# Two gate projections cut into twelve pieces and set between the products of a chunk scan

## What is computed

```python
q_a, k_a, v_a, z_a, b_a, a_a, q_b, k_b, v_b, g_a, g_b = split(h @ w_in)
o_a = gated_delta_rule(l2norm(silu(conv(q_a))), l2norm(silu(conv(k_a))), silu(conv(v_a)), g, beta)
o_a = rmsnorm(o_a, gdn_norm_w) * silu(z_a)
o_b = sliding_window_sink_attention(rope(q_b), rope(k_b), v_b, sinks)
y = sigmoid(g_a) * (o_a @ w_a_out) + sigmoid(g_b) * (o_b @ w_b_out)
x = x + gt1 * (y @ w_mix_out)
...
def step(state, chunk):            # the chunk scan: 4 chunks of 64 tokens, 4 heads
    v_new = u_c - w_c @ state
    o = qd @ state + a_c @ v_new
    state = state * exp(gl) + kd.T @ v_new
```

## Time and profile before

| | |
|---|---|
| time, median of 3 runs | 1943.98 us (1943.7 to 1944.88) |
| profiled execution | 1944.16 us |
| its span (first to last record) | 1942.4 us |
| mean clock of TensorE | 0.971 of full speed |
| PE busy | 1794.1 us, 92% |
| PEld busy | 1494.5 us, 77% |
| DVE busy | 1513.9 us, 78% |
| ACT busy | 1085.4 us, 56% |
| chain that ended last | PE 76%, DVE 13%, ACT 6%, issue 3% |

### The profile page before, as it was taken

One profiled execution on the slowest core, in us unless ns is written; L12 is line 12 of the kernel. 1 busy time (PEld: TensorE's weight loads), 2 busy tenths in 40 slices (PEclk: granted clock), 3 DMA queues, 4 the chain that ended last, 5 costly groups with the idle time before them and its releaser, 6 DMA issues.

```text
span 1942.4 us, 25749 instructions
## 1 busy us (share of the span) xinstructions
PE 1794.1 (92%) x9708; PEld 1494.5 (77%) x9708; DVE 1513.9 (78%) x1475; ACT 1085.4 (56%) x917; POOL 88.6 (5%) x139
## 2 busy tenths in 40 slices
PE   3988998899998989998799999999999999999996
PEld 1877877788887878876587787877878778788785
DVE  6768937977756667446788898898988989888888
ACT  2563215433333472232677777777777777877774
POOL 4010000000000010001000000000000010000100
PEclk9999989999999999898899999999999999999999
DMA  9525744788873414224699999999999999999994
GB/s 302 179 87 183 230 129 152 245 297 301 279 243 109 152 44 109 85 71 148 245 375 352 387 355 370 364 359 378 355 373 372 357 372 365 360 378 364 352 370 174
DMA packets 261719, 520.78 MB, mean 268 GB/s; under 512 B 12202, under 2 KB 75924, under 8 KB 261652
## 3 DMA queue, kind: packets, MB, share of 16 engines
q1 hardware_dynamic: 257988, 506.21, 73.7%
q0 software_dynamic: 3664, 13.63, 1.8%
HBM read 511.42 MB, written 8.39 MB: 268 GB/s over the span
## 4 chain that ended last, share of the span: by engine, by line
PE 76%; DVE 13%; ACT 6%; issue 3%; SPq 1%; DMA 0%; DVEq 0%; ACTq 0%
PE bank L964 17%; PE bank L965 17%; PE bank L966 17%; PE bank L970 6%; PE bank L971 5%; PE bank L972 5%; DVE w_lo L1508 2%; DVE ada_acc L1529 2%; DVE w_lo L2042 2%; ACT w_hi L933 2%; PE bank L1456 1%; PE bank L984 1%; ACT w_hi L691 1%; PE bank L1229 1%; PE bank L1203 1%
## 5 line engine op out<-in xcount | busy, mean ns | idle before, releaser
L2042 DVE TENSOR_TENSOR w_lo<-ring,w_hi 128x2048 fp32r<-128x2048 f32 x336 | 768.3, 2291 | 118.2 <-ACT w_hi L933 114.8
L933 ACT CAST w_hi<-ring 128x2048 fp32r<-128x2048 f32 x336 | 640.0, 1910 | 131.7 <-PE bank L966 131.6
L964 PE MATMUL bank<-w_hi,xg_hi 128*128 128x512 f32 x896 | 358.6, 400 | 23.1 <-DVE w_lo L2042 23.1
L966 PE MATMUL bank<-w_hi,xg_lo 128*128 128x512 f32 x896 | 353.8, 395 | 0.0
L965 PE MATMUL bank<-w_lo,xg_hi 128*128 128x512 f32 x896 | 353.8, 395 | 0.0
L970 PE MATMUL bank<-hT_hi,w_hi 128*128 128x256 f32 x960 | 282.3, 294 | 12.9 <-DVE w_lo L1508 6.3
L1508 DVE TENSOR_TENSOR w_lo<-ring,w_hi 128x2048 fp32r<-128x2048 f32 x96 | 219.5, 2290 | 87.5 <-ACT w_hi L691 87.3
L971 PE MATMUL bank<-hT_lo,w_hi 128*128 128x256 f32 x960 | 274.7, 286 | 0.0
L972 PE MATMUL bank<-hT_hi,w_lo 128*128 128x256 f32 x960 | 274.4, 286 | 0.0
L691 ACT CAST w_hi<-ring 128x2048 fp32r<-128x2048 f32 x96 | 182.3, 1901 | 81.7 <-PE bank L966 45.5
L964 PEld LDWEIGHTS bank<-w_hi,xg_hi 128*128 128x128 f32 x896 | 168.8, 188 | 67.6 <-issue 21.2
(11 more groups left out here) (393 smaller groups left out, 2071.4 us busy)
## 6 DMA issues: line engine op xcount, KB each, us to landing
ring<-in_moe_w_gate_dram SPq DMA_DIRECT2D x112, 1024.0 KB, 7.1
ring<-in_moe_w_up_dram SPq DMA_DIRECT2D x112, 1024.0 KB, 7.4
ring<-in_moe_w_down_dram SPq DMA_DIRECT2D x112, 1024.0 KB, 7.4
ring<-in_ada_w_dram SPq DMA_DIRECT2D x48, 1024.0 KB, 5.6
ring<-in_w_in_dram SPq DMA_DIRECT2D x38, 1024.0 KB, 5.1
ring<-in_ffn_w_gate_dram SPq DMA_DIRECT2D x14, 1024.0 KB, 6.3
ring<-in_ffn_w_up_dram SPq DMA_DIRECT2D x14, 1024.0 KB, 5.1
ring<-in_ffn_w_down_dram SPq DMA_DIRECT2D x14, 1024.0 KB, 5.4
```

The lines of the kernel that those rows point to most:

```text
L933: act.copy(w_hi[p % NS_MOE][:], ring[:, p % RING, :]).then_inc(hi_ready, 1)
L964: pe.matmul(o, xh, wh, start=start, stop=False)
L966: return pe.matmul(o, xl, wh, start=False, stop=stop)
L2042: dve.tensor_tensor(w_lo[p % NS_MOE][:], ring[:, p % RING, :], f32(w_hi[p % NS_MOE][:]), ALU.subtract).then_inc(taken, 1)
```

## The change

Gates 6 and 7 are cut into twelve pieces (`gate_piece`) of 9 or 6 matmuls. Eight stand in the scan, one or two for each chunk, and four behind it; `wb 0` now stands wholly behind the scan. The two outputs of gates 6 and 7 go to banks 0 and 3 instead of both to bank 0, which shifts the banks of `wb 1`, the mix product and `gate_row`. The output products of a chunk are no longer alternated: a small product of zeros clears the bank, then come the four from the state and the four from `v_new`. On VectorE and ScalarE the splits move: gate 7's stands ahead of the scan, `wb 0`'s behind it, `wa 0`'s on ScalarE behind the rounding of `oa_hi`. In layer 0 the last six adaLN units move from between gates 5, 6 and 7 to behind `wb 0`, `wb 1` and `wa 0`, and with them their passes, their small products, `ada_turn` and `gate_diag`. `gate_row` moves from ahead of `wa 0` to between the two halves of the mix product, `gate_copy` behind the splits. On ScalarE a table set that holds both Ln and Exp is loaded ahead of them, twice in each mixer.

```diff
@@ units @@
             if l == 0:
-                ada_units(1 if j < 3 else 2)
+                ada_units((1, 1, 1, 2, 2, 0, 0, 0)[j])
         for cc in range(2):
             units.append((("wb", l, cc), True))
+            if l == 0:
+                ada_units(2)
         for cc in range(2):
             units.append((("wa", l, cc), True))
+            if l == 0 and cc == 0:
+                ada_units(2)
@@ ScalarE @@
+                act.preload_act_table_set("natural_log_exp_and_others")
...
+                ahead(("gate", l, 7), 0)
                 for n in range(NCH):
...
-                    if n == 0:
-                        ahead(("gate", l, 7), 0)
-                    if n in (1, 2):
-                        gate(5 + n)
-                        ahead(("wb", l, 0), 0)
...
+                    if n == 2:
+                        gate(6)
                 act.wait_ge(o_s, NCH * (l + 1))
                 act.activation(o_sq, OT, ACT.Square).then_inc(osq_s, 1)
-                if l == 0:
-                    ada_copy(2, 1)
+                ahead(("wb", l, 0), 0)
+                act.wait_ge(split_used, s_of[("gate", l, 7)] + 1)
+                act.activation(gate_sb[:, 14:16, :].rearrange("p a b -> p (a b)"),
+                               ps[3][:], ACT.Sigmoid).then_inc(gate_s, 1)
                 ahead(("wb", l, 1), 0)
+                act.preload_act_table_set("natural_log_exp_and_others")
                 act.wait_ge(on_ps, l + 1)
...
                 act.activation(o_r, o_r, ACT.Exp, scale=-0.5).then_inc(on_s, 1)
-                ahead(("wa", l, 0), 0)
                 act.wait_ge(oaf, l + 1)
                 act.copy(oa_hi[:], OT).then_inc(oa_h, 1)
+                ahead(("wa", l, 0), 0)
                 ahead(("wa", l, 1), 0)
+                if l == 0:
+                    ada_copy(2, 1)
@@ TensorE @@
+                def gate_piece(i):
+                    late, piece = divmod(i, 6)
+                    t, third = divmod(piece, 3)
+                    wh, wl = parts(("gate", l, 6 + late), KO)
+                    if piece == 0 and not late:
+                        pe.wait_ge(gate_s, 8 * l + 6)
+                    for ko in ((0, 1, 2), (3, 4, 5), (6, 7))[third]:
+                        ins = by_channel(ps[(0, 3)[late]][:, t * T:(t + 1) * T], wh[:, ko, t * P:(t + 1) * P],
+                                         wl[:, ko, t * P:(t + 1) * P], hT_hi[:, ko, :], hT_lo[:, ko, :],
+                                         ko == 0, ko == KO - 1)
+                    if piece == 5:
+                        ins.then_inc(split_used, 1)
...
-                        meanwhile(0)
+                        gate_piece(2 * n)
...
-                    meanwhile(1)
+                    gate_piece(2 * n + (n > 0))
...
+                    if n:
+                        pe.matmul(ps[7][:, 0:T], zero_b[:, 0:P], zero_b[:], start=True, stop=False)
+                        for h in range(H):
+                            pe.matmul(ps[7][:, h * CHUNK:(h + 1) * CHUNK], state[:, h, :], qT[:, h, here],
+                                      start=False, stop=False)
                     for h in range(H):
-                        o = ps[7][:, h * CHUNK:(h + 1) * CHUNK]
-                        if n:
-                            pe.matmul(o, state[:, h, :], qT[:, h, here], start=True, stop=False)
-                        ins = pe.matmul(o, v_new[rows, h, :], AT[rows, tb * H + h, rows], start=n == 0, stop=True)
+                        ins = pe.matmul(ps[7][:, h * CHUNK:(h + 1) * CHUNK], v_new[rows, h, :],
+                                        AT[rows, tb * H + h, rows], start=n == 0, stop=n == 0 or h == H - 1)
                     ins.then_inc(o_ps, 1)
-                    if l == 0 and n in (0, 2):
-                        ada_piece(0, 9 + n // 2, 1, False, False)
+                    if n == 0:
+                        gate_piece(1)
+                gate_piece(8)
+                gate_piece(9)
 
                 pe.wait_ge(osq_s, l + 1)
...
+                gate_piece(10)
+                gate_piece(11)
+                half_branch("wb", 0, (2, 3), ob_hi, ob_lo, 0)
                 pe.wait_ge(gate_s, 8 * (l + 1))
+                half_branch("wb", 0, (2, 3), ob_hi, ob_lo, 1)
                 if l == 0:
-                    pe.wait_ge(ada_s, 2)
-                branch("wb", 1, (0, 1), ob_hi, ob_lo)
-                pe.wait_ge(yb_s, 4 * l + 1)
-                gate_row(2 * l + 1, m_dg, (2, 3))
+                    ada_piece(0, 9, 1, False, False)
+                half_branch("wb", 1, (0, 5), ob_hi, ob_lo, 0)
+                pe.wait_ge(ln2_s, 2 * (l + 1))
+                half_branch("wb", 1, (0, 5), ob_hi, ob_lo, 1)
+                if l == 0:
+                    ada_piece(0, 10, 1, False, False)
                 pe.wait_ge(oa_s, l + 1)
                 branch("wa", 0, (6, 7), oa_hi, oa_lo)
...
+                        if kh == 0 and cc == 1:
+                            gate_row(2 * l + 1, m_dg, (3, 1))
@@ VectorE @@
+                ahead(("gate", l, 7), 0)
                 for n in range(NCH):
...
-                    if n == 0:
-                        ahead(("gate", l, 7), 0)
...
-                        if n == 1:
-                            ahead(("wb", l, 0), 0)
...
                 ahead(("wb", l, 0), 0)
-                if l == 0:
-                    ada_columns(2, 0, 1, NQA, NQ)
-                    dve.wait_ge(ada_s, 2)
                 dve.wait_ge(gate_s, 8 * (l + 1))
                 dve.wait_ge(o_ps, NCH * (l + 1))
-                gate_diag(2 * l + 1, l, 2, m_dg)
+                ahead(("wb", l, 1), 0)
                 gated(1, 0, (2, 3), y_sum[:, 0:4, :])
-                ahead(("wb", l, 1), 0)
...
-                gate_copy(2 * l + 1, m_gt, (2, 3))
...
+                if l == 0:
+                    ada_columns(2, 0, 1, NQA, NQ)
+                    dve.wait_ge(ada_s, 2)
+                gate_diag(2 * l + 1, l, 2, m_dg)
+                ahead(("mix", l, 1, 1), 0)
+                gate_copy(2 * l + 1, m_gt, (3, 1))
```

More of the change, by code:

```diff
@@ L187, in build_program @@
         am1 = sb("am1", [P, 2 * P], BF16)
+        zero_b = sb("zero_b", [P, T], BF16)
         cols = sb("cols", [P, 2 * P])
@@ L584, in _ @@
             pool.memset(prm_b, 0.0).then_inc(zeroed, 1)
+            pool.memset(zero_b[:], 0.0)
             pool.memset(eps_c[:], EPS)
@@ L840, in gate @@
                 def gate(j):
-                    product(("gate", l, j))
+                    product(("gate", l, j), 1 if j < 6 else 0)
                     act.activation(gate_sb[:, 2 * j:2 * j + 2, :].rearrange("p a b -> p (a b)"),
@@ L1255, in _ @@
                     state = states[n % 2]
-                    def meanwhile(t):
-                        if n in (1, 2):
-                            if t == 0:
-                                pe.wait_ge(gate_s, 8 * l + 5 + n)
-                            one_block(("gate", l, 5 + n), 0, t)
-                        if n == 3:
-                            half_branch("wb", 0, (2, 3), ob_hi, ob_lo, t)
                     if n > 0:
@@ L1307, in _ @@
                 ins.then_inc(on_ps, 1)
+                gate_piece(10)
+                gate_piece(11)
+                half_branch("wb", 0, (2, 3), ob_hi, ob_lo, 0)
                 pe.wait_ge(gate_s, 8 * (l + 1))
+                half_branch("wb", 0, (2, 3), ob_hi, ob_lo, 1)
                 if l == 0:
-                    pe.wait_ge(ada_s, 2)
-                branch("wb", 1, (0, 1), ob_hi, ob_lo)
-                pe.wait_ge(yb_s, 4 * l + 1)
-                gate_row(2 * l + 1, m_dg, (2, 3))
+                    ada_piece(0, 9, 1, False, False)
[4 more added lines that the diff above has]
+                    ada_piece(0, 10, 1, False, False)
                 pe.wait_ge(oa_s, l + 1)
                 branch("wa", 0, (6, 7), oa_hi, oa_lo)
-                branch("wa", 1, (4, 5), oa_hi, oa_lo)
+                if l == 0:
+                    ada_piece(0, 11, 1, False, True)
+                half_branch("wa", 1, (4, 5), oa_hi, oa_lo, 0)
                 pe.wait_ge(yb_s, 4 * l + 2)
-                pe.wait_ge(gt_s, 2 * l + 1)
+                half_branch("wa", 1, (4, 5), oa_hi, oa_lo, 1)
+                if l == 0:
+                    ada_turn(2, 1)
                 for kh in range(2):
@@ L1325, in _ @@
                                 ko = 4 * kh + kk
-                                ins = by_token(ps[2 * cc + tb][:], hT_hi[:, ko, tokens(tb)], hT_lo[:, ko, tokens(tb)],
+                                ins = by_token(ps[(0, 2, 6, 7)[2 * cc + tb]][:], hT_hi[:, ko, tokens(tb)], hT_lo[:, ko, tokens(tb)],
                                                wh[:, kk, :], wl[:, kk, :], ko == 0, ko == KO - 1)
@@ L1852, in _ @@
                 dve.tensor_tensor(oa_lo[:], OT, f32(oa_hi[:]), ALU.subtract).then_inc(oa_s, 1)
-                gated(1, 1, (0, 1), y_sum[:, 4:8, :])
+                gated(1, 1, (0, 5), y_sum[:, 4:8, :])
                 ahead(("wa", l, 1), 0)
```

(3 more changed lines are left out.)

4 lines of the change are left out of this document (removed).

## The result

| | before | changed |
|---|---|---|
| median | 1943.84 us (1942.19 to 1944.88, 4 runs) | 1918.06 us (1917.06 to 1918.78, 4 runs) |
| span of the profiled execution | 1942.4 us | 1916.5 us |
| mean clock of TensorE | 0.971 | 0.980 |

The ratio is 0.9869 (95%: 0.9857 to 0.9881), 25.8 us less. I had said 1933, in a range of 1923 to 1939, so the kernel is 4.9 us faster than the range allowed.

What follows compares the result with a forecast made beforehand. The two mixers bound it: TensorE delayed by too-thick filling in the scans, then ScalarE and VectorE behind them. Layer 1 -5.0, layer 0 -3.4 and table loads -2.6 made -11.0 us: 1933 us, range 1923 to 1939.

Steps and rivals of the forecast that it cites:

- two falls in each scan: Both layers' scans: TensorE's clock falls twice in each as before, 1.5 us each, so 3.0 per scan.
- The fall at 821: Layer-1 scan before the change: clock at 1.2 GHz for 3.2 us without idle time ahead, taken as evidence against rival A.
- Rival A: Clock stays up in filled scans with denser outputs; five to six falls saved, -20 us, 1924; chance 0.25.
- The one fall in each tail: Idle time ahead of wa 0 and layer 0's gaps waiting for VectorE cost one clock fall each, 1.5 us.
- Prices: Scan products at full clock: output group 2.3 us (2.91 before), state product 1.31; chunk 7.87 instead of 14.2.
- The ends of the tails: Layer 0: mix product at 314.0, VectorE's chain ending at 312; layer 1: 12.2 us from wa 0, plus 1.5 for the clock.
- Table loads: Normalisation: Ln and Exp in one set take one 1.28 us load per mixer off the path, 2.6 us in all.
- the second load lies beside VectorE's two passes: Normalisation: the other removed load, that of L784, is hidden, so only 1.28 us per mixer counts.
- the new wait of 4.5 us: Layer 1's tail: TensorE waits 4.5 us before wa 0, whose split now stands behind ScalarE's rounding.
- VectorE as the bound of layer 0's tail: Layer 0 behind the scan: moved adaLN passes, splits and other VectorE work make 36.3 us; mix product at 309, not 319.1.
- Rival B: Layer 0 gives nothing, through weight transfers landing late or a longer VectorE chain: -6 to -7 us, 1937; chance 0.15.
- Rival C: Scan mostly at 1.2 GHz because thin pieces leave TensorE less dense: 1967, middling case some 1950; chance 0.04.

Runs made afterwards that it cites:

- three small moves: Changed kernel with wa 0's split ahead of the rounding, layer 1's gate row ahead of wa 0, two adaLN pairs in layer 0's scan: 1907.4 us together.
- One program: Changed kernel with output products alternated by head again, without the zero product: 1935.08 us, ratio 0.9959, ten runs.

## Why the prediction was wrong in size

The side, the places and the new waits came as forecast. The sum was -11.0 and the spans differ by 25.9. The missing 14.9 us, in spans, by its own steps (15.1 by the rounded parts):

1. **The clock (the step that failed): 6.0 in the scans.** I took two falls in each scan at 1.5 each, because "update, outputs and state product ... remain the sort of work after which the clock fell". None came. The fall at 821 followed the alternated outputs, not these products as such: grouped outputs alone take it away with everything else as before, and alternated outputs bring falls back in scans without idle time. Rival A described the right case for the scans, at 0.25, but its -20 took the tails' falls away too, and those came; with only the four falls of the scans gone it would have said 1927. The runs add that filling is the second condition: without it grouped outputs don't hold the clock. The one fall in each tail came as forecast; from wa 0 to the mix product layer 1 took 14.3 us, where 12.2 and 1.5 were forecast, and 11.9 without the fall, so that one cost 2.4.
The Trainium skill ("TensorE: Matmul & The Clock Gate", HAM oscillation) puts such falls down to idle gaps. The unfilled scans here agree (0.61 in the window of the version without filling), though their gaps of 0.67 and 0.78 us are much shorter than the waits for transfers in the page's example; the scan with alternated outputs doesn't (0.90 with TensorE busy throughout). I took the row at 821 as evidence against the rule for the changed kernel, and it was evidence about an order of products that the change removes.
2. **Prices: 1.5 in layer 1, 1.8 in layer 0, 3.3 together.** Outputs 2.09 instead of 2.3, the state product 1.02 instead of 1.31 (its old price carried the start of the fall at 821), three times each. In layer 0 the same shows in the start of VectorE's chain, 33.0 us behind the first value product (267.34 - 234.34); my sum had 34.8, and 3.0 for the clock on top.
3. **The ends of the tails: 0.9.** VectorE's chain was 36.5 us (forecast 36.3), but the mix product began 0.5 us behind it, not the 2.0 that I gave wa 1 at the low clock. Layer 1's was 0.6 longer than forecast (14.3 for 13.7).
4. **Table loads: 2.0.** I took one load per mixer as on the path; 1.8 and 2.7 us came. The step "the second load lies beside VectorE's two passes" was nearly right: by the rows above all the removed loads give 1.4 and 1.7 us, of which the second is 0.1 and 0.4. What the sum left out is TensorE's clock between there and the scan, 1.0 us or a little more in layer 1. The price of a load was right: 1.28, and Ln starts 0.01 us behind it (818.79 + 1.28 to 820.08); the Trainium skill's longer price for a switch ("ScalarE: Activation LUTs", What ACT_TABLE_LOAD costs: 2.66 us with its drain) doesn't show in the trace. It would have forecast these two stretches (5.3 for 4.6) nearly right, but by luck: only 3.1 of the 4.6 came through the loads.
5. **Elsewhere: 2.9.** 1.6 ahead of layer 0's normalisation and 1.3 in the experts, where the programs are alike. The start of Ln in layer 0 lies between 113.9 and 116.9 us in the profiled executions, of changed and unchanged kernels alike, so this part belongs to single executions; the medians differ by nearly the same 25.8, so what of it is lasting stays open.

Right were the new wait of 4.5 us (4.52), `gate_row` at 1.7 per layer (1.75 and 1.78), VectorE as the bound of layer 0's tail, and pieces that cover their waits (no idle mark in the scan). Rival B's transfers played no part: no TensorE or VectorE wait in layer 0's tail names a DMA, and the one of ScalarE that does is 0.19 us. Rival C's state exists, but in the unfilled version: 1953, near the 1950 given for its middling case.

What holds the clock was tried by two undoings, of the order and of the filling. That it is the change of weight shape from head to head, rather than the 64 columns or the missing zero product, was not tried and stays open.

## What to carry to other kernels

Filling between short products has two sizes to meet: thick enough to cover each wait, thin enough not to delay the chain. No filling at all cost 35 us here, and blocks of 24 in two chunks with none in the other two cost 17, both through the clock as well. When a clock fall has no idle time ahead of it, look at which order of products precedes it, and whether the change keeps that order, before counting it again. And when work is moved behind the bound stretch, read the other engines' order there at once: three small moves of that kind gave another 10.7 us.

## What I had not expected of the hardware

A scan in which TensorE has no idle time can still run at 0.90 of the clock (alternated 128-row and 64-row products of 64 columns), and the same work in groups at 1.00. One program, ten times on one chip, took 1925.6 to 1945.3 us at mean clocks of 0.977 to 0.965, while the changed kernel's four runs stayed within 1.7 us. In seven profiled executions with grouped outputs and thin pieces one of the 14 scans had a fall, so the state is robust, but not certain.
